# A chunked RWKV-7 recurrence: chunk matrices as 64x64 blocks in opposite corners of TensorE's array

## The reference, cut to what matters

```
def step(S, inp):
    r_t, w_t, k_t, v_t, a_t, b_t = inp
    sa = jnp.einsum('bhij,bhj->bhi', S, a_t)
    S = S * w_t[:, :, None, :] + sa[..., None] * b_t[:, :, None, :] + v_t[..., None] * k_t[:, :, None, :]
    return S, jnp.einsum('bhij,bhj->bhi', S, r_t)
```

## Time and profile before

| | |
|---|---|
| median of 3 runs | 947.8 us (947.59 to 948.4) |
| profiled execution: its time, its span | 949.6 us, 947.9 us |
| TensorE matmul busy | 840.9 us, 89% of the span |
| VectorE, ScalarE, GpSimd busy | 432.1, 219.6, 70.6 us |
| mean granted TensorE clock | 0.934 |

### The profile page before, as it was taken

One profiled execution on the slowest core, in us unless ns is written; L12 is line 12 of the kernel. 1 busy time (PEld: TensorE's weight loads), 2 busy tenths in 40 slices (PEclk: granted clock), 3 DMA queues, 4 the chain that ended last, 5 costly groups with the idle time before them and its releaser, 6 DMA issues. The chain is left out here.

```text
span 947.9 us, 14552 instructions
## 1 busy us (share of the span) xinstructions
PE 840.9 (89%) x5559; PEld 604.8 (64%) x5559; DVE 432.1 (46%) x960; ACT 219.6 (23%) x445; POOL 70.6 (7%) x69
## 2 busy tenths in 40 slices
PE   3599999999999999999999997974669999999985
PEld 2367787787787787877976876631356564555441
DVE  3133564555555556547546546886230212322314
ACT  3121422423414404405314322101100000000002
POOL 0000000000000000000000003990000000000000
PEclk9889999999999999999999998995756999999998
DMA  9934323324224223224124223012399999999992
GB/s 275 233 88 115 111 68 93 89 66 123 71 75 115 66 66 115 66 66 137 44 68 136 76 80 131 1 68 93 102 421 400 419 418 419 418 419 418 418 407 77
DMA packets 108512, 167.61 MB, mean 177 GB/s; under 512 B 7505, under 2 KB 91691, under 8 KB 95804
## 3 DMA queue, kind: packets, MB, share of 16 engines
q1 hardware_dynamic: 104780, 158.96, 47.4%
q0 software_dynamic: 1664, 4.98, 1.4%
q10 hardware_dynamic: 2032, 3.18, 1.2%
HBM read 158.68 MB, written 8.43 MB: 176 GB/s over the span
## 5 line engine op out<-in xcount | busy, mean ns | idle before, releaser
L274 PE MATMUL bank<-room,wall 128*128 128x264 f32 (+1 forms) x1152 | 291.7, 400 | 26.2 <-ACT thw L792 14.1
L274 PEld LDWEIGHTS bank<-room,wall 128*128 128x128 f32 x1152 | 214.9, 194 | 74.0 <-issue 19.1
L1539 PE MATMUL bank<-G,xn 128*128 128x128 f32 (+1 forms) x384 | 74.6, 328 | 3.0 <-DVE G L1760 3.0
L1539 PEld LDWEIGHTS bank<-G,xn 128*128 128x128 f32 (+1 forms) x384 | 56.9, 204 | 19.3 <-issue 6.5
L1567 PE MATMUL bank<-ring,xg 128*32 128x256 f32 x1024 | 61.1, 399 | 4.3 <-DMA ring<-in_expert_w_up_dram 3.4
L1567 PEld LDWEIGHTS bank<-ring,xg 128*32 128x32 f32 x1024 | 36.2, 115 | 30.5 <-issue 13.0
L274 PE MATMUL bank<-wall,merged 128*128 128x512 f32 (+1 forms) x96 | 45.2, 619 | 2.7 <-DVE merged L1312 2.5
L1597 PE MATMUL bank<-ysb,SW 128*128 128x512 f32 (+1 forms) x96 | 45.6, 610 | 1.0 <-DVE ysb L1799 1.0
L1587 PE MATMUL bank<-ring,hT 128*32 128x512 f32 x256 | 35.8, 710 | 4.9 <-ACT hT L1655 4.9
L1776 DVE TENSOR_TENSOR x<-x,bank 128x512 f32<-128x512 f32 (+1 forms) x48 | 32.8, 684 | 14.7 <-PE bank L1597 14.7
L1769 DVE COPY xg<-bank 128x512 f32<-128x512 f32 x8 | 5.5, 691 | 71.8 <-PE bank L1539 71.8
(11 more groups left out here) (364 smaller groups left out, 1311.8 us busy)
## 6 DMA issues: line engine op xcount, KB each, us to landing
wall<-in_w_in_dram SPq DMA_DIRECT2D x72, 512.0 KB, 3.9
ring<-in_expert_w_gate_dram SPq DMA_DIRECT2D x32, 1024.0 KB, 26.5
ring<-in_expert_w_up_dram SPq DMA_DIRECT2D x32, 1024.0 KB, 19.7
ring<-in_expert_w_down_dram SPq DMA_DIRECT2D x32, 1024.0 KB, 26.1
room<-in_state_ret_dram SPq DMA_DIRECT2D x8, 512.0 KB, 4.8
out_ret_s_dram<-room POOLq DMA_DIRECT2D x8, 512.0 KB, 3.4
wall<-in_w_out_dram SPq DMA_DIRECT2D x8, 512.0 KB, 3.5
room<-in_state_rwkv_dram SPq DMA_DIRECT2D x1, 2048.0 KB, 8.5
```

The costliest lines, as they stand in the source:

```text
L274: return nc.tensor.matmul(out, lhsT, rhs, start=start, stop=stop, skip_group_check=loose)
L1539: last = mm(XG[kk // 4][:, (kk % 4) * P:(kk % 4 + 1) * P], xn[rows(tt), tt, kk * P:(kk + 1) * P], G[q % 2][rows(tt), tt].rearrange("p e s ...
```

## The change: what it does

Each pair's 128x128 matrix is replaced by its two diagonal 64x64 blocks, held as one [128, 64] tile: chunk 0 on partitions 0 to 63, chunk 1 on 64 to 127. Each matmul of 128x128 becomes two of 64x64, one in the upper left and one in the lower right corner of the array (`by_chunk`); both write one bank, on different partitions. Buffers, masks and copies of these matrices are half as wide. `x0` and the Horner results keep 128 columns and get buffers of their own. `w1` leaves the matmul that it shared with `at4` and stands behind `a4`. In q and y the four blocks of array and chunk are used, in two banks each (`QB`, `YB`). The products `ar` with `bt` go to banks 2 and 3 instead of 4 and 5, and wait there for `o_root` in place of the token copies. `settle` is a wait on a semaphore that has long been set.

```diff
+    s, t = np.meshgrid(np.arange(P) % C, np.arange(C), indexing="ij")
+    m = np.zeros((P, 4, C))
+    lo = np.zeros((P, 2, C))
...
+        QB, YB = (M[2], M[0]), (M[3], M[1])
+        def by_chunk(pe, out, lhsT, rhs_):
+            for u in range(4):
+                for ps in HALF:
+                    last = mm(pe, out(ps, u), lhsT(ps, u), rhs_(ps, u), True, True)
+            return last
...
+                for t in range(TT):
+                    for m, src in ((0, bt), (2, kt)):
+                        for par in range(2):
+                            at = slice(t * P + par * C, t * P + par * C + C)
+                            for h, hs in enumerate(HALF):
+                                last = mm(pe, M[h][HALF[par], (4 * t + m) * C:(4 * t + m + 2) * C], src[hs, at], ar[hs, t, :, par * C:par * C + C], True, True)
+                last.then_inc(sem("prod"), 1)
+                settle(pe)
                 past(pe, "o_root", n)
...
-                for u in range(4):
-                    last = mm(pe, v4(M[0])[:, u, :], pr[:, u, 0, :], la[:, u, 0, :], True, True)
-                last.then_inc(sem("a2_mm"), 1)
+                by_chunk(pe, lambda ps, u: c4(M[0])[ps, u, :], lambda ps, u: pr[ps, u, 0, :], lambda ps, u: la[ps, u, 0, :]).then_inc(sem("a2_mm"), 1)
...
-                    last = mm(pe, M[2 + u // 2][:, (u % 2) * 2 * P:(u % 2 + 1) * 2 * P], a2[:, u, :], at2w[:, u].rearrange("p a b -> p (a b)"), True, True)
-                last.then_inc(sem("at4w1_mm"), 1)
+                by_chunk(pe, lambda ps, u: c4(M[2])[ps, u, :], lambda ps, u: a2[ps, u, :], lambda ps, u: at2w[ps, u, 0, :]).then_inc(sem("at4_mm"), 1)
+                by_chunk(pe, lambda ps, u: c4(M[0])[ps, u, :], lambda ps, u: at2w[ps, u, 0, :], lambda ps, u: a2[ps, u, :]).then_inc(sem("a4_mm"), 1)
+                by_chunk(pe, lambda ps, u: c4(M[3])[ps, u, :], lambda ps, u: a2[ps, u, :], lambda ps, u: at2w[ps, u, 1, :]).then_inc(sem("w1_mm"), 1)
...
             def horner(src, bank, ready):
                 past(pe, ready, n)
-                for u in range(4):
-                    last = mm(pe, v4(bank)[:, u, :], nt[:, u, :], src[:, u, :], True, True)
-                last.then_inc(sem("horner_mm"), 1)
+                by_chunk(pe, lambda ps, u: v4(bank)[ps, u, :], lambda ps, u: nt[ps, u, :], lambda ps, u: src[ps, u, :]).then_inc(sem("horner_mm"), 1)
...
-                    last = mm(pe, M[2][hs, t * P:(t + 1) * P], zf[:, u, 0:HD], pr[:, u, 1, :], True, True, True)
+                for t in range(TT):
+                    for par in range(2):
+                        for h in range(2):
+                            last = mm(pe, QB[par][HALF[h], t * C:(t + 1) * C], zf[HALF[par], 2 * t + h, 0:HD], pr[HALF[par], 2 * t + h, 1, :], True, True, True)
...
-                for u in range(4):
-                    dve.wait_ge(sem("prod"), n * 6 + (u - 5))
-                    last = V.tensor_tensor(pr[:, u], v4(M[u]), mk[:], mult)
+                dve.wait_ge(sem("prod"), n * 2 - 1)
+                for h in range(2):
+                    last = V.tensor_tensor(pr[:, h::2], M[h][:].rearrange("p (t m c) -> p t m c", t=TT, m=4),
+                                           mk[:].unsqueeze(1).broadcast_to([P, TT, 4, C]), mult)
```

More of the change, by code:

```diff
@@ L545, in pe_pass @@
                     last.then_inc(sem("tok_mm"), 1)
+                for t in range(TT):
[6 more added lines that the diff above has]
+                settle(pe)
                 past(pe, "o_root", n)
                 for t in range(TT):
[L549 to L560, removed]
+                    for par in range(2):
+                        at = slice(t * P + par * C, t * P + par * C + C)
+                        for h, hs in enumerate(HALF):
+                            last = mm(pe, M[2 + h][HALF[par], t * C:(t + 1) * C], ar[hs, t, 0, par * C:par * C + C], bt[hs, at], True, True)
+                last.then_inc(sem("prod"), 1)
             if front:
@@ L602, in pe_pass @@
                 past(pe, "a4_copy", n)
[L603 to L608, removed]
+                by_chunk(pe, lambda ps, u: c4(M[5])[ps, u, :], lambda ps, u: at4w[ps, u, 0, :], lambda ps, u: a4[ps, u, :]).then_inc(sem("a8_mm"), 1)
+                by_chunk(pe, lambda ps, u: c4(M[1])[ps, u, :], lambda ps, u: a4[ps, u, :], lambda ps, u: at4w[ps, u, 1, :]).then_inc(sem("w2_mm"), 1)
                 meanwhile(1)
@@ L616, in pe_pass @@
             if back:
+                settle(pe)
                 past(pe, "a8_copy", n)
                 past(pe, "w2_ready", n)
-                for u in range(4):
-                    last = mm(pe, v4(M[2])[:, u, :], a8[:, u, :], w2s[:, u, :], True, True)
-                last.then_inc(sem("w3_mm"), 1)
+                by_chunk(pe, lambda ps, u: c4(M[2])[ps, u, :], lambda ps, u: a8[ps, u, :], lambda ps, u: w2s[ps, u, :]).then_inc(sem("w3_mm"), 1)
                 meanwhile(2)
@@ L625, in pe_pass @@
             if back:
+                settle(pe)
                 past(pe, "w3_ready", n)
                 past(pe, "rhs_ready", n)
[L629 to L634, removed]
+                by_chunk(pe, lambda ps, u: c4(M[3])[ps, u, :], lambda ps, u: la[ps, u, 1, :], lambda ps, u: w3[ps, u, :]).then_inc(sem("nt_mm"), 1)
+                by_chunk(pe, lambda ps, u: v4(M[4])[ps, u, :], lambda ps, u: w3[ps, u, :],
+                         lambda ps, u: rhs[ps, u].rearrange("p a b -> p (a b)")).then_inc(sem("x0_mm"), 1)
                 meanwhile(3)
@@ L684, in pe_pass @@
                     last.then_inc(sem("fg_mm"), 1)
[L685 to L689, removed]
+                for part in range(2):
+                    for t in range(TT):
+                        for par in range(2):
+                            for h in range(2):
+                                u, ps, hs = 2 * t + h, HALF[par], HALF[h]
+                                value = tmk[ps, t, 2, hs] if part else zf[ps, u, HD:P]
+                                last = mm(pe, YB[par][hs, t * C:(t + 1) * C], value, pr[ps, u, 3 if part else 1, :], part + t == 0, False, True)
+                last.then_inc(sem("y_part_mm"), 1)
             if front:
@@ L699, in pe_pass @@
                         past(pe, "ft_ready", n)
+                        past(pe, "y_part_mm", n)
                     t, par = c // 2, c % 2
@@ L797, in act_pass @@
                 past(act, "a2_mm", n)
-                A.copy(a2[:], v4(M[0])).then_inc(sem("a2_copy"), 1)
+                A.copy(a2[:], c4(M[0])).then_inc(sem("a2_copy"), 1)
                 past(act, "lakv_mm", n)
                 A.copy(rhs[:, :, 1, :], M[4][:, 0:4 * HD].rearrange("p (u c) -> p u c", u=4)).then_inc(sem("rhs_ready"), 1)
[L801 to L804, removed]
+                past(act, "at4_mm", n)
+                A.copy(at4w[:, :, 0, :], c4(M[2])).then_inc(sem("at4_copy"), 1)
                 past(act, "a4_mm", n)
-                A.copy(a4[:], v4(M[0])).then_inc(sem("a4_copy"), 1)
+                A.copy(a4[:], c4(M[0])).then_inc(sem("a4_copy"), 1)
             if front:
@@ L831, in act_pass @@
                 past(act, "y_mm", n)
-                A.copy(ys[:, 0:TP], M[3][:, 0:TP]).then_inc(sem("y_copy"), 1)
+                for par in range(2):
+                    last = A.copy(ys[:, 0:TP].rearrange("p (t a c) -> p t a c", t=TT, a=2)[:, :, par, :],
+                                  YB[par][:, 0:TT * C].rearrange("p (t c) -> p t c", t=TT))
+                last.then_inc(sem("y_copy"), 1)
                 past(act, "zt_mm", n)
@@ L943, in dve_pass @@
                 past(dve, "w0_ready", n)
-                past(dve, "at4_copy", n)
-                for half in range(2):
-                    us = slice(2 * half, 2 * half + 2)
-                    last = V.tensor_tensor(at4w[:, us, 1, :], M[2 + half][:].rearrange("p (u a c) -> p u a c", u=2, a=2)[:, :, 1, :], at2w[:, us, 1, :], add)
-                last.then_inc(sem("w1_ready"), 1)
+                past(dve, "w1_mm", n)
+                V.tensor_tensor(at4w[:, :, 1, :], c4(M[3]), at2w[:, :, 1, :], add).then_inc(sem("w1_ready"), 1)
                 meanwhile(0, 1)
@@ L968, in dve_pass @@
                 past(dve, "w2_ready", n)
[L969 removed]
+                V.tensor_tensor(w3, c4(M[2]), w2s, add).then_inc(sem("w3_ready"), 1)
                 meanwhile(2, 3)
@@ L1009, in dve_pass @@
                 past(dve, "q_mm", n)
-                V.tensor_tensor(q[:].rearrange(c2, t=TT), M[2][:, 0:TP].rearrange(c2, t=TT), ar[:, :, 1, :], add).then_inc(sem("q_ready"), 1)
+                for par_ in range(2):
+                    ps = HALF[par_]
+                    last = V.tensor_tensor(q[:].rearrange(c2, t=TT)[:, :, ps], QB[par_][:, 0:TT * C].rearrange(c2, t=TT), ar[:, :, 1, ps], add)
+                last.then_inc(sem("q_ready"), 1)
                 for par_ in range(2):
```

87 lines of the change are left out of this document (39 added, 48 removed).

## The result

The changed kernel takes 941.03 us (median of 5 runs, 938.42 to 941.42) against 947.59 (5 runs, 945.72 to 948.4): a ratio of 0.9927, 95% interval 0.9904 to 0.9951. It is faster, by 6.6 us where some 17 were forecast; the time lies at the upper end of the range, 921 to 942. The profiled execution took 941.42 us, with a span of 939.7.

What follows compares the result with a forecast made beforehand. TensorE's stream in the loop was taken to bound the kernel, the last pass waiting on VectorE. 13.6 (seven passes) + 4.4 (tail) + 0.5 (prologue) - 1.6 (clock) = 16.9 us won, giving 931 us, range 921 to 942.

Steps and rivals of the forecast that it cites:

- The prices of the groups: TensorE's matmul groups in each loop pass: eight 64-column matmuls take 0.46 us for 0.89; 128 columns win nothing.
- visit: Going from 128x128 matmuls to 64x64 tiles and back, paid once by each of eight groups a pass: 0.34 us.
- q to y: End of each loop pass, tiles before and after: 16 + 48 + 32 passes at 0.029 us, won 0.4 us.
- the fourth rival: Four blocks run at once in q and y, with the tail at its cap: 925 us; chance 10%.
- The first: Pairs run singly because two tiles on one bank wait for each other: near 993 us; chance 4%.
- the second rival: Dearer tile runs and visits leave the loop about where it was, tail some 3 us: 945 us; chance 12%.
- I count one more such fall, +1.6 us: Loop, behind the `thw` wait: faster products idle TensorE longer, so one more drop to 1.2 GHz, costing 1.6 us.
- the third rival: Clock falls to 1.2 GHz behind TensorE's idle stretch in six passes instead of one: near 939 us; chance 14%.
- The products at nothing: Products ahead of the `thw` wait cost nothing either way; they are hidden, and faster ones lengthen the wait.
- The tail: Last pass: VectorE's last step of the samples' states comes 4.4 us earlier, bounds 0 and 6.
- GpSimd's own share ends at 639.52 whatever happens: Last pass: GpSimd's end stays fixed, 6.2 us before VectorE's, so up to 6.2 us can be won.
- The prologue's: Ahead of the first pass: smaller constants `mk` and `mlo`, 0.2 MB less to load, won 0.5 us.

Runs made afterwards that it cites:

- the stand-in work: Changed kernel with four unused 128x128 matmuls of 264 columns on TensorE ahead of `r`'s projection, in the wait for `thw`; 921.32 us, ratio 0.9751.
- the slower products: Changed kernel with the products as 64x128 matmuls as before: 928.15 us, 0.9812; or with the products for `pr` done twice: 927.37 us, 0.9801.
- the earlier `thw`: Changed kernel with ScalarE's square `kks` moved behind `tha`, so `thw` no longer waits for VectorE; 906.91 us, ratio 0.9584.

## Why the prediction was right on the groups and wrong on the clock

**What bounds the kernel** was read rightly: time that left TensorE's stream in the loop shortened an undisturbed pass, from 67.93 to 65.30 us.

**The prices of the groups held.** A group with its visit takes, from half projection to half projection and with the 0.2 us by which the neighbouring half projection grew (1.98 for 1.78), 1.74 (A), 1.75 (B), 1.28 (C), 0.81 (D), 1.69 (E) and 1.23 (h1), forecast 1.73, 1.73, 1.27, 0.80, 1.67 and 1.21. The visit of 0.34 us came out of one state step between two projections, and up to 0.2 of it is paid in the projections, not in the group. From `r`'s projection to q a pass without a fall (with the stand-in work) is 1.67 us shorter than before; the forecast has 1.94 less 0.4.

**q to y was too small.** The step "16 + 48 + 32 passes at 0.029 ... won 0.4" counted two tiles at a time; the stretch won 0.96, and these two, 1.67 and 0.96, are the 2.63 us of a pass. The 16 passes of q alone are issued in 0.29 us (134.82 to 135.11), where two at a time would take 0.46. So the fourth rival's mechanism, four blocks at once, is what happened. The first and the second rival are out: the two matmuls of a pair of A write one bank and start 0.007 us apart, and the pairs follow each other by 0.061. The Trainium skill, TensorEngine Tiling (Array Packing), section Restrictions and Gotchas, says that different row tiles cannot access the same PSUM bank at the same time. The trace disagrees for tiles that write different partitions of it.

**The step that failed is the clock:** "I count one more such fall, +1.6 us", and with it the 14% for the third rival. It was said that "faster products lengthen the wait"; that is what they did, but as a second wait, since the chain to `thw` had not moved:

```profile
232.32 0.45 PE L274 MATMUL bank<-ar,bt 64*64 64x128 f32 x8
...
233.25 0.41 PE L274 MATMUL bank<-bt,ar 64*64 64x64 f32 x16
233.59 0.71 PE L274 MATMUL bank<-lwa,wst_w 64*128 64x264 f32 x2
234.99 0.71 PE L274 MATMUL bank<-lwa,wst_w 64*128 64x264 f32 x2 [0.69 <-DVE kx L893]
237.63 6.77 PE L274 MATMUL bank<-room,wall 128*128 128x272 f32 x16 [1.93 <-ACT thw L802]
244.33 1.15 PE L274 MATMUL bank<-x 64*64 64x64 f32 x32
```

Between the products and `r`'s projection TensorE stands idle twice, and the clock falls in seven passes of seven. In the kernels with packed groups `r`'s projection takes 3.86 us where nothing falls; here it takes 5.35 and 5.55 in the first two passes and 6.70 to 6.82 in the other five. That is 17.8 us more in all, against 1.58 (5.35 for 3.77) for the one fall before. So the term is +16.2 and not +1.6. I had weighed six passes that did not fall with 1.93 us of idle time as evidence that they would not with more. That was weak evidence: the kernel before without GpSimd's part, whose loop is the same, has two falls in seven. Not even the third rival had the right price: it took every fall at 1.6.

**The products at nothing** is the same error from the other side: they were hidden, and the cover was named, but shortening hidden work on the engine that waits is not free where its clock depends on that work. The fill, the slower products and the earlier `thw` show it three ways.

**The tail** won 2.4 us of 4.4, inside the bounds of 0 and 6, by terms that came out otherwise. Up to the samples' first step it won 5.70 where 4.9 were forecast: "half of it at the lower clock" was misread, since the granted clock is 0.50 over the whole 5.15 us from group A to B before, and the same stretch now takes 2.28. Behind that step it lost 3.3 where 0.5 were forecast. "GpSimd's own share ends at 639.52 whatever happens" failed: it ends at 635.81, and slows VectorE and is slowed by it. What the forecast gave as the reason for its lower bound, that VectorE "only meets more of GpSimd's work", is what happened to those 3.3 us.

**The prologue's** 0.5 us can't be told from how runs differ there.

The sum with the measured terms: 7 x 2.63 = 18.4 won in the passes, 2.4 in the tail, 16.2 lost to the clock, 4.6 us in all; the other 3.6 of the profiled executions' 8.2 are the start and the experts' phase, where the change can't be told from how runs differ. That the time still lies in the range, 1 us from its end, is luck: more was won in the passes than forecast and the start came earlier, and both together made up for about half of a clock term that was ten times too small.

## What to carry to other kernels

Before shortening work that lies hidden ahead of a wait on TensorE, look at the granted clock behind that wait: one fall in seven passes was the sign here, and less work there cost 16.2 of the 20.8 us that were won elsewhere. Take the wait away first (here two ScalarE lines in another order), or put other work into it. And pack 64x64 blocks into the corners only where the matmuls become narrower too: with 64 columns a group of four won half its time, with 128 it only paid the visit.

## What the runs showed of the hardware

Four 64x64 fp32 tiles, two in each pair of opposite corners, run at once: the products' eight passes of 128 columns are issued in 0.22 us (232.59 to 232.81, shown below) where two passes at a time would take 0.44 by the 0.11 us a pass of the earlier trace rows.

```profile
232.59 0.40 PE L274 MATMUL bank<-ar,kt 64*64 64x128 f32 x8
232.81 0.40 PE L274 MATMUL bank<-ar,bt 64*64 64x128 f32 x8
```

A fall of the clock comes in two sizes in these profiles: `r`'s projection loses 1.5 to 1.7 us (before, and the first two passes after) or 2.8 to 3.0 (the other five).
